# A two-layer block kernel on one core: rotary tables computed later, halved products behind a norm, two stores per staged unit, and a new table of places

## What is computed

```python
def first_block(x, ...):
    h = rmsnorm(x, norm1_g)
    p = einsum('bsd,de->bse', h, w_in)          # u (256), q,k,v of 4 differential heads, q,k,v of 4 stick-breaking heads
    a_out = pool_mixer(u, pool_w, pool_scale)
    b_out = diff_attention(dq, dk, dv, lam, lam_init, diff_norm_g)
    c_out = stick_breaking_attention(sq, sk, sv, sb_norm_g)
    x = x + einsum('bse,ed->bsd', concat([a_out, b_out, c_out]), w_out)
    h2 = rmsnorm(x, norm2_g)
    x = x + einsum('bsf,fd->bsd', silu(h2 @ w_gate) * (h2 @ w_up), w_down)
    return rmsnorm(x, final_norm_g)

def hybrid_layer(x, c, positions, w_ada, ...):   # second layer: gmlp and retention branches
    mod = silu(c) @ w_ada + b_ada
    h = rmsnorm_2(x, g_pre) * (1 + scale) + shift
    gu, gv, gg, rq, rk, rv, rg = split(h @ w_in)
    y = concat([gmlp_branch(gu, gv, gg, ...), retention_branch(rq, rk, rv, rg, positions, ...)])   # rotary(q), rotary(k)
    return x + gate * rmsnorm_2(y @ w_out, g_post)
```

## Time and profile before

| | |
|---|---|
| median of 3 runs | 3701.42 us (3700.64 to 3703.38) |
| the profiled execution | 3704.28 us, span 3702.5 us |
| mean granted TensorE clock | 0.987 of full speed |
| PE, DVE, ACT, POOL busy | 97%, 52%, 45%, 22% of the span |
| DMAs | 763.90 MB, 328579 packets |

### The profile page before, as it was taken

How to read it: one execution, slowest core, us unless ns; L and a number is a source line. 1 busy time by engine, 2 the same in 40 slices (tenths; PEclk the granted TensorE clock), 3 DMA queues, 4 the chain that set the end, 5 groups by cost and what they waited for, 6 DMA issues and landing times.

```text
span 3702.5 us, 50185 instructions
## 1 busy us (share of the span) xinstructions
PE 3589.6 (97%) x18900; PEld 3064.6 (83%) x18900; DVE 1913.0 (52%) x4043; ACT 1663.8 (45%) x3393; POOL 804.4 (22%) x704
## 2 busy tenths in 40 slices
PE   7899999899999999999999999999999999999999
PEld 6788888787887888888888898888888888888788
DVE  4255654666657755445646555435478752111443
ACT  4344545445665554545544444435455542111322
POOL 3344343444454332000011001110000000000100
PEclk9999999999999999999999999999999999999999
DMA  6787677778776768555555556454454465555454
GB/s 188 219 252 223 192 219 259 267 273 291 253 266 224 242 216 298 179 172 190 176 173 177 172 211 214 160 198 165 165 213 147 148 231 183 191 182 205 172 191 155
DMA packets 328579, 763.90 MB, mean 206 GB/s; under 512 B 53393, under 2 KB 204945, under 8 KB 272018
## 3 DMA queue, kind: packets, MB, share of 16 engines
q1 hardware_dynamic: 267538, 725.02, 56.5%
q10 hardware_dynamic: 60800, 35.67, 3.5%
HBM read 586.25 MB, written 174.35 MB: 205 GB/s over the span
## 4 chain that ended last, share of the span: by engine, by line
PE 84%; DVE 6%; ACT 3%; DMA 3%; issue 1%; POOL 1%; ACTq 1%; SPq 1%; DVEq 0%
PE PS L1503 23%; PE PS L1505 23%; PE PS L1504 23%; PE PS L1622 3%; PE PS L1632 3%; PE PS L1614 2%; PE PS L1613 2%; PE PS L1646 2%; DMA XS<-in_w_ada 1%; POOL WF L2529 1%; ACTq L1861 1%; PE PS L1581 1%; DMA GROW<-in_gmlp_ln_g 1%; DVE BIG L2109 1%; ACT WF L1749 0%
## 5 line engine op out<-in xcount | busy, mean ns | idle before, releaser
L1503 PE MATMUL PS<-BIG,WF 128*128 128x512 f32 (+1 forms) x1792 | 687.4, 384 | 11.5 <-ACT BIG L1815 4.6
L1505 PE MATMUL PS<-BIG,WF 128*128 128x512 f32 (+1 forms) x1792 | 675.9, 377 | 0.0
L1504 PE MATMUL PS<-BIG,WF 128*128 128x512 f32 (+1 forms) x1792 | 675.7, 377 | 0.0
L2529 POOL TENSOR_TENSOR WF<-RAW,WF 128x512 fp32r<-128x512 f32 x380 | 507.5, 1360 | 631.1 <-ACT WF L1749 631.0
L1503 PE MATMUL PS<-WF,BIG 128*128 128x512 f32 (+1 forms) x1656 | 608.3, 367 | 7.6 <-DVE BIG L2098 4.6
L1505 PE MATMUL PS<-WF,BIG 128*128 128x512 f32 (+1 forms) x1656 | 592.4, 358 | 0.0
L1504 PE MATMUL PS<-WF,BIG 128*128 128x512 f32 (+1 forms) x1656 | 591.6, 357 | 0.0
L1503 PEld LDWEIGHTS PS<-BIG,WF 128*128 128x128 f32 x1792 | 342.5, 191 | 71.5 <-ACT BIG L1815 6.0
L1505 PEld LDWEIGHTS PS<-BIG,WF 128*128 128x128 f32 x1792 | 341.8, 191 | 63.0
L1504 PEld LDWEIGHTS PS<-BIG,WF 128*128 128x128 f32 x1792 | 342.6, 191 | 58.0
L1869 ACT ACTIVATE PP<-PS,SM 128x512 f32<-128x512 f32 (+3 forms) x320 | 198.9, 623 | 375.1 <-DVE SM L2194 364.2
(11 more groups left out here) (233 smaller groups left out, 6244.5 us busy)
## 6 DMA issues: line engine op xcount, KB each, us to landing
WF<-scratch_WS SPq DMA_DIRECT2D x264, 1024.0 KB, 5.0
scratch_WS<-WF SPq DMA_DIRECT2D x110, 1024.0 KB, 6.7
W<-scratch_WS SPq DMA_DIRECT2D x66, 1024.0 KB, 5.0
RAW<-in_w_in SPq DMA_DIRECT2D x84, 512.0 KB, 4.4
KV<-scratch_KS SPq DMA_DIRECT2D x60, 512.0 KB, 6.0
QQ<-scratch_QS SPq DMA_DIRECT2D x192, 128.0 KB, 5.3
XH<-in_x SPq DMA_DIRECT2D x32, 512.0 KB, 7.3
scratch_QS<-STG ACTq DMA_DIRECT2D x96, 128.0 KB, 4.0
```

The costliest lines, as they stand in the source:

```text
L1503: pe.matmul(o, Ah, Bh, start=first, stop=False)
L1504: pe.matmul(o, Ah, Bl, start=False, stop=False)
L1505: return pe.matmul(o, Al, Bh, start=False, stop=last)
L2529: pool.tensor_tensor(lo, rawp(n)[:, 512 * i:512 * i + 512], hi.bitcast(F32), ALU.subtract).then_inc(*inc("w_lo", ("w_lo", n, i)))
```

## The change

Five edits:

1. The four steps of the rotary tables stand behind blocks 4 to 7 of column 0 instead of 1 to 4 (the v block counts as two).
2. `gw_steps` gets one turn more, in block 2 of column 0, so that the first `load_gw` is issued two blocks sooner and each later turn comes one place sooner.
3. The first block behind a norm does its products by halves of the pieces: k = 0 to 3 for both outputs, then k = 4 to 7 for both, and the turning of the second token group is put between them.
4. The layouts of the staging buffers and of the scratch tensor QS are changed, so that one unit of q, k or v is stored by 2 DMAs instead of 4 (q, k) or 8 (v of the stick-breaking heads). The bytes are the same. The elementwise instructions that fill the buffers are as many and as large as before; for q and v they write with a stride.
5. The table of places is new in most of its lines (1484 digits and 742 half steps, as before).

```diff
 HALF_STEPS = (
-    "0000000000000000000000000000000000000000000000001200110120000010020002001100100000000200000100101210"
+    "0000000000000000000000000000000000000000000000001002100000101002000101020010020001100010101001101010"
...
@@ f_block, the part for first
+                lower, upper = range(4), range(4, 8)
                 for f, (u, b, before) in enumerate(banks):
-                    do(("gemm_f", u, w, f, 0, range(8), b, before, rd))
-                    if f and not ready:
+                    do(("gemm_f", u, w, f, 0, lower, b, before, rd))
+                yield 2.9
+                if ready:
+                    flush(0, (0, 1))
+                for f, (u, b, _) in enumerate(banks):
+                    do(("gemm_f", u, w, f, 0, upper, b, (), rd))
+                    if not f and not ready:
                         flush(0, (0, 1))
-                    yield 2.9
-                    if ready and not f:
-                        flush(0, (0, 1))
-                flush(2, (2, 3))
+                yield 2.9
+                flush(2, (2, 3) if ready else (2,))
                 split_half()
                 for f, (u, b, _) in enumerate(banks):
-                    do(("gemm_f", u, w, f, 1, range(8), b, (), rd))
+                    do(("gemm_f", u, w, f, 1, lower, b, (), rd))
+                    if not f and not ready:
+                        flush(0, (3,))
+                yield 2.9
+                for f, (u, b, _) in enumerate(banks):
+                    do(("gemm_f", u, w, f, 1, upper, b, (), rd))
                     done("do", f, u, b)
-                    yield 2.9
+                yield 2.9
@@ at_block
-            if c == 0 and n in (1, 2, 3, 4):
-                do((("load_positions", "angles", "rotary_tables", "store_tables")[n - 1],))
+            if c == 0 and n in (4, 5, 6, 7):
+                do((("load_positions", "angles", "rotary_tables", "store_tables")[n - 4],))
@@ projections
-                    if nblk >= 1 and (c, nblk) >= (0, 4) and not (both and i % 2):
+                    if (nblk >= 1 and (c, nblk) >= (0, 4) and not (both and i % 2)) or (c, nblk, i) == (0, 2, 0):
                         next(gw, None)
@@ put_qk
-                for a, src in enumerate(stage(s)):
-                    for r in range(2):
-                        rows = src[64 * r:64 * r + 64, :].bitcast(F32)
-                        if kind == "q":
-                            act.dma_start(QS[ft, 4 * c:4 * c + 4, :, a, r, :].rearrange("q d t -> d q t"), ...)
-                        else:
-                            act.dma_start(KS[ft, c, 64 * a:64 * a + 64, r, :], rows)...
+                for r in range(2):
+                    rows = stage_parts(s)[64 * r:64 * r + 64, :].bitcast(F32)
+                    if kind == "q":
+                        act.dma_start(QS[ft, 4 * c:4 * c + 4, :, r, :].rearrange("q d x -> d q x"), ...)
+                    else:
+                        act.dma_start(KS[ft, c, :, r, :].rearrange("(a d) t -> d a t", a=2), ...)
@@ put_v
-                for a, src in enumerate(stage(s)):
-                    for f in range(2):
-                        ...
-                        for i in range(2):
-                            act.dma_start(by_head[:, 2 * g + i, :, a, :], ...)
+                view = stage_parts(s).rearrange("p (i f x) -> p i f x", i=2, f=2).bitcast(F32)
+                for f in range(2):
+                    act.dma_start(VS[f, c, :, 2 * g:2 * g + 2, :, :].rearrange("p i a e -> p i (a e)"), view[:, :, f, :])...
@@ store_v of ACT (the DVE side and q alike)
-                to = stage(s)[0] if ft == 4 else stage(s)[0].bitcast(F32)
-                act.activation(to, PS[b][:, :], ACT.Copy)...
+                if ft == 4:
+                    act.activation(stage_v(s)[0], PS[b][:, :].rearrange("p (m e) -> p m e", m=8), ACT.Copy)...
```

More of the change, by code:

```diff
@@ new lines @@
+    "2112010011020013500200022001110001101011101101012110120000000011210020100101100011001001401200000001"
+    "1100011001011000211010010000010222100201000000010000100201001220221012000000000010001000112020020100"
+    "1110022110202460310100000200000000010020010001100100030110101120101000001000200002000201001000011001"
+    "0031112210112000002000000000000110100001000200102224102202020000020211110000001000000000001001000011"
+    "0010002010010020020000020001011201101000100000202120000020000201000000020002100100000100000100000000"
@@ new lines @@
+    "2100200011001100001000000201010020011002010101021000002110010001102201121153201000000010100000011000"
+    "1011102000101001000000000011002000101002000200002101210211100011010000020001001100011000210111002200"
+    "1102021000021001002000001020010000101000100012102100111000000120000000000111100101000001024301112122"
+    "0000011200002000100001000000001001000011000102000001012100001000000000200100001000011120021000000000"
+    "1000000100000101011000011010011010010000210110011000010200020102000001000001010200010010202011022000"
@@ L236 @@
+    "0001100202120100100200100000000001200010111122002200200110000000200210000001100010000101011211302400"
+    "1000000001010010200011001100100012012112001011100011000010010000200200000010010100021220002020010001"
+    "0100001001010110011100010000211210010001000001000000000000000000000001000000000201000200200110210010"
+    "000003010112001110100200001210100000000010210011000010211001020020100300100200101025"
 )
@@ L1439, in stage, with stage_parts, stage_q, stage_v @@
             return STG[:, 1024 * s:1024 * s + 512], STG[:, 1024 * s + 512:1024 * s + 1024]
+        def stage_parts(s):
+            return STG[:, 1024 * s:1024 * s + 1024]
+        def stage_q(s):
+            q4 = stage_parts(s).rearrange("p (q a t) -> p q a t", q=4, a=2)
+            return q4[:, :, 0, :], q4[:, :, 1, :]
+        def stage_v(s):
+            m8 = stage_parts(s).rearrange("p (m a e) -> p m a e", m=8, a=2)
+            return m8[:, :, 0, :], m8[:, :, 1, :]
         def keys_of(kb):
@@ L1610, in scores @@
                 kk = keys_of(ks).rearrange("p (r t) -> p r t", r=2)
-                qq = queries(q).rearrange("p (a r t) -> p a r t", a=2, r=2)
+                qq = queries(q).rearrange("p (r a t) -> p a r t", a=2, r=2)
                 o = PS[4 + b][:, 0:w]
@@ L1822, in store_qk @@
                     on.wait_ge(*e)
-                act.activation(stage(s)[0], PS[b][:, :], ACT.Identity,
-                               scale=0.125 if kind == "q" else 1.0).then_inc(*inc("qkv_hi", ("qh", u)))
+                if kind == "q":
+                    act.activation(stage_q(s)[0], PS[b][:, :].rearrange("p (q t) -> p q t", q=4), ACT.Identity,
+                                   scale=0.125).then_inc(*inc("qkv_hi", ("qh", u)))
+                else:
+                    act.activation(stage(s)[0], PS[b][:, :], ACT.Identity).then_inc(*inc("qkv_hi", ("qh", u)))
             def store_v(c, u, b, s, sbefore, ft, g):
@@ L1829, in store_v @@
                     on.wait_ge(*e)
-                to = stage(s)[0] if ft == 4 else stage(s)[0].bitcast(F32)
-                act.activation(to, PS[b][:, :], ACT.Copy).then_inc(*inc("qkv_hi", ("qh", u)))
+                if ft == 4:
+                    act.activation(stage_v(s)[0], PS[b][:, :].rearrange("p (m e) -> p m e", m=8), ACT.Copy).then_inc(
+                        *inc("qkv_hi", ("qh", u)))
+                else:
+                    act.activation(stage(s)[0].bitcast(F32), PS[b][:, :], ACT.Copy).then_inc(*inc("qkv_hi", ("qh", u)))
             def put_u(c, u, s, f):
@@ L2832 @@
     scr = {}
-    for name, shape in (("QS", [6, 16, 64, 2, 2, 128]), ("KS", [6, NC, 128, 2, CT]), ("VS", [2, NC, 128, 4, 2, 128]), ("VW", [4, NC, 128, 4, 128]),
+    for name, shape in (("QS", [6, 16, 64, 2, 256]), ("KS", [6, NC, 128, 2, CT]), ("VS", [2, NC, 128, 4, 2, 128]), ("VW", [4, NC, 128, 4, 128]),
                         ("US", [2, 128, S + 16]), ("YS", [S, D]), ("GP", [1, D]), ("GWS", [128, 4, 128]), ("WS", [SPLIT - KEPT, 128, 2048]), ("TB", [2, 128, 1024])):
```

46 lines of the change are left out of this document (19 added, 27 removed).

## The result

The changed kernel takes 3644.67 us (median of 4 runs, 3643.57 to 3645.83); the kernel before, beside it on the same chip, 3702.40 (3700.64 to 3706.45, 4 runs). The ratio is 0.9844, interval 0.9831 to 0.9856: 57.7 us less. 3661.3 was forecast, with 3639 to 3687 as the range.

The account below looks back on a forecast made before the run. PE, busy 3589.6 of 3702.5 us, bounds the kernel; only idle time and low clock could be won. 27.7 idle, 10.9 clock and 1.5 of Part 3 make 40.1: 3664.2 from the profiled 3704.3, less 2.9 gives 3661.3, range 3639 to 3687.

Parts of the forecast that it names:

- The sum: Gains of 27.7 us idle time, 10.9 of clock and 1.5 of Part 3: 40.1 us in all.
- Idle time and clock: At five places of the input projections 27.7 of 36.2 us idle go; of the low clock's 16.4 us, 10.9.
- Part 4: V stores on ACT at column borders: 0.55 us an issue, bursts shrink 11.6 and 3.3 us, waits behind nearly go.
- issue is paid otherwise: Rival, 5%: the fewer, larger stores hold ACT as long at the column borders; 20 us lost, 3681 us.
- Part 1: At 74 us, later rotary tables free DVE and ACT: 7.3 us of PE waits gone, 0.5 taken as remaining.
- The tables stall a new place: Rival, 10%: DVE's 12 us or ACT's 5 in the v block delay a bank; 3673 us.
- Part 2: At the first gmlp matrix in column 0, the sooner load ends PE's 3.23 us wait, remaining 0.
- Part 3: 72 instead of 24 products before first scores at 148 us, queries' 5.01 nearly gone; gates 0 to 3, 1.5 taken.
- Part 5: New table of places: nothing in the rows prices it; 0 taken, bounds of 10 us to either side.
- the places also clear later waits: Rival, 14%: outside the five stretches of the input projections, 16 us more goes, a little clock included; 3643 us.
- The signs of being wrong: Wrong if: v store issue ≥2 us; idle after 600 us +20; new column-0 wait >4. Expected: ≤2 low stretches before 600.
- Slower: Rival, 4%: new places make PE's scores wait for an exponential's bank; 7 us a collision, twelve give 3745.

Follow-up runs that it names:

- a_no_gw: Changed kernel with the first gmlp load back in block 4, the tables still late: 3645.78 us.
- a_no_halves: Changed kernel with whole pieces again behind the norms: 3652.49 us.
- a_no_tables: Changed kernel with the rotary tables back behind blocks 1 to 4, the early gmlp load kept: 3653.11 us.
- a_whole_col0: Changed kernel with whole pieces only in the first block of column 0 and in column 0's gate 0: 3648.39 us.
- a_8_stores: Changed kernel with each v store cut into four by partitions, 8 issues a unit, same layout, bytes and 1 KB pieces: 3675.44 us.
- b_tables: Kernel before with only the later rotary tables and the sooner first gmlp load added: 3689.68 us.
- b_halves: Kernel before with only the products by halves of pieces added: 3707.64 us.
- a_no_places: Changed kernel with the old table of places: 3662.83 us.
- b_places: Kernel before with only the new table of places added: 3714.32 us.
- b_stores_tables: Kernel before with the new stores, later rotary tables and sooner gmlp load, but old places and whole pieces: 3662.6 us.
- a_no_stores: Changed kernel with the old staging and stores, 4 or 8 for each unit: 3687.98 us.

## Why the prediction was right, and where its steps were not

**The sum.** 40.1 us were forecast with the places at 0. The nearest kernel to that is the changed one with the old places: 3702.97 - 3662.83 = 40.1 us, so what was missed in the total is the term of the places. That the two agree to the tenth is luck, since steps inside the sum went wrong in both directions. Two of its remainders do not follow from its own terms either: 0.6 with the 1.05 behind it is 1.65 and not 1.5, and the 0.5 at 566 us became 1.0 without a reason given. Together they shift the sum by 0.35 us.

**Idle time and clock.** Forecast for this part: 27.7 + 1.5 us of idle time and 10.9 of clock. Measured over the first five windows: 50.2 us of idle time became 20.1, so 30.2 gone. The low clock cost 32.80/2 = 16.4 in the earlier trace rows and costs 10.07/2 = 5.0 now: 11.4 gone. Both terms held in size; the way of counting the clock, half of PE's busy time in the low stretches, also closes the balance of the whole span to 3.4 us (19.0 of 22.4). Three low stretches are left before 600 us instead of at most two, but they are of 3.4 us each.

The Trainium skill (TensorE: Matmul & The Clock Gate, Terms) takes half of the whole throttled time: by its rule the six low stretches of before would have cost an estimate of 22.2 us and the three of after 5.1. The two agree for stretches in which PE is busy throughout, as 3.40 of 3.40 are at 585 us; for those of before, where PE was idle for a quarter, the page's figure lies 5.8 us above what the busy time gives.

**Part 4** was right in mechanism, and in price at three borders of four. The bursts there shrank as worked out (by 12.3 and 4.0 us, against 11.6 and 3.3), and the waits of the earlier trace rows are gone. At the end of column 3 the price of 0.55 us an issue failed: four issues took 6.1 us, one of them 2.90. The prediction had named 2 us for one issue of the new v store as a sign of being wrong, and by that sign this step fails there. It cost 1.95 us of waiting and the low clock behind it; the traces of a_no_gw and a_no_halves show the same burst (6.05 and 6.22 us for the four), those of a_no_tables and a_whole_col0 do not, and why single issues are dear there stays open. What the step also did not see is that a burst's length also decides what a table of places may do: the stores are worth 28 us alone and 43 in company. The rival "issue is paid otherwise" is refuted by two runs: 256 KB are issued as fast as 64 (0.49 and 0.50 us), and a_8_stores, with as many issues as before and a quarter of the pieces in each, takes 0.46 us for one and keeps 31 of the 43 us of loss.

**Part 1** was right: 7.3 us of idle time and more with the clock, 14.6 us up to product 168 in b_tables. "The tables stall a new place" did not happen: PE is without a wait from 24 to 139 us. b_tables as a whole gains 12 us in the median; whether it gives 2 of the 14.6 back later is not clear of the spread of its runs (3684 to 3696).

**Part 2** was the wrong step. The 3.23 us at the first gmlp matrix are gone without it (a_no_gw). Where the load is written did not matter: the loads ahead of it on SP waited for POOL, which stood still for 18.68 us behind ACT, and by the trace of before that was itself an effect of the tables. One cause had been counted as two parts; the sum did not suffer, since both parts were made.

**Part 3** failed as argued. It was to put 72 instead of 24 products ahead of the scores; it puts 24, and b_halves still waits 4.93 us for the queries. The count of 72 comes from the table. In the gates it was argued that the gain is nearly given back, and that holds in size: the four waits of column 3's gate 0 were 0.82, 0.57, 1.55 and 0.16 us, 3.1 together; after they are 2.50 and 0.56, 3.1 too. It does not hold in kind. The second output was to cover the 0.82 us; instead its products start four pieces sooner and PE waits 2.50 us for their PSUM bank, which DVE's addition of the sum before it (line 2311) frees only then. Its 8 us exist only with the new places. I did not find one wait that carries them; the difference to a_no_halves lies in several small ones and in the clock behind them.

**Part 5** was the mis-sized term: 0 with bounds of 10, where a_no_places says 18. Of the difference between these two traces, 10.1 us lie between products 168 and 840, where idle time falls from 14.1 to 7.0, so at the column borders, among them the 4.41 us for the queries. That was foreseeable: the same order listing from which I read the 72 products was of the changed kernel with both parts, and the second token group's exchange with the exponentials stood in it as well; I took them for part 3's and priced the table at nothing. Another 8.2 us of the difference lie behind product 1008, where idle time differs by 3.4; that window is between 2893.0 and 2903.4 us long in the traces of all 14 kernels, so that nearly half of what the places are worth here cannot be laid on any one wait.

**The rival "the places also clear later waits"** gave 3643, and the time came out at 3644.67, but the places are not shown to be its cause. Behind product 840 the changed kernel gained 14.6 us, 10.5 of them in the sixth window, where the wait of 5.93 us for the modulation's weights fell to 1.53. But a_no_places, with the old table, has 1.73 there. With whole pieces, the wait falls to 1.94 when the table is new (b_places) and stays at 5.85 when it is old (b_stores_tables). So the new table is enough, and so are the halves on top of the stores and tables, though not the halves alone (6.49 in b_halves). What shifts the weights' arrival stays open. The last 4.1 us are spread over 2900 us and are mostly clock (idle time there 48.8 before, 49.4 after), which differs as much between kernels with nearly the same idle time there: 2895.3 us in b_stores_tables and 2903.4 in a_no_places (52.7 and 52.8 idle), which differ only in the halves.

**The signs of being wrong.** Besides the dear issue above, there are three low stretches before 600 us where at most two were to come. The others held: no new wait of over 4 us in column 0, and less idle time behind product 840 than before (56.8 us against 62.6).

**Slower** by new collisions (4%) was real as a mechanism: b_places shows it, though not as it was put. PE waited for activations behind the store burst, not for an exponential's bank. With part 4 in, there is no such burst.

## What to carry to other kernels

A hand-made order of work is tuned to the stalls that it was made around. The same table cost 13 us with long store bursts and gave 18 with short ones, so price an order only together with the change that it comes with, and make it anew when a stall goes. When two waits stand near each other, ask whether the first delays the second's cause on another queue before a separate edit is credited with it. And count DMAs, not bytes, on an engine that also does the work others wait for: 8 issues instead of 2 cost 31 us here through one in-order engine that is busy for only 46%.

## What the runs showed that was not expected

The issues of one burst are not equally dear. Most take 0.4 to 0.6 us, single ones 1.2 to 3.2 (the longest in a_no_halves). In a_no_stores four in a row of 2.67, 2.20, 2.24 and 1.23 us make the burst at the border of columns 0 and 1 long; in the changed kernel it is one of 2.90 us at 518. Neither the length of the burst nor the pieces explain it: 14 in a row cost 0.65 us each with 256-byte pieces (a_no_stores) and 0.67 with 1 KB pieces (a_8_stores). What does stays open.

The low clock can follow a very short wait. In the changed kernel, PE's waits of 1.49 and 1.53 us (starts of the work behind them 654.07 and 689.46) look alike, and only the second is followed by the 1.2 GHz level (690.8 to 694.2). A third, again of 1.53 us (the work behind it starts at 755.94), is followed by none:

```profile
654.07 1.02 PE L1684 MATMUL PS<-SM,XS 128*128 128x1 f32 x8 [1.49 <-issue]
...
689.46 1.02 PE L1684 MATMUL PS<-SM,XS 128*128 128x1 f32 x8 [1.53 <-DVE XS L2337]
```

```profile
690.80:694.20 3.40, 3.40 (x15) 3.21 (x14) 2.60 (x4) 1.88 (x10) 2.81 (x2) 0.50 1.01 416
652.00:660.00 8.00, 6.51 (x40) 5.51 (x39) 2.77 (x6) 2.53 (x5) 5.70 (x5) 1.00 1.00 354
```

The number of low stretches differs from kernel to kernel by more than their waits do: a_whole_col0 is idle for 76.6 us and the changed kernel for 76.8, yet the one has 8 low stretches of 29.4 us together and the other 12 of 45.0. Single effects under 5 us could not be told apart for that reason.
